# The query multiplication of the first 14 gathered key tiles moved from VectorE to GpSimd

## The reference, cut to what matters

```python
idx = indexer_topk(qi, wi, ki_all, qpos, n_keep)            # n_keep = 256 per sample token
k_sel = jnp.where(is_new, take_rows(k, ni), cache_k[phys, off].astype(k.dtype))
...
logits = jnp.einsum('bqhd,bqkhd->bqhk', q, k_sel).astype(jnp.float32) * ATTN_SCALE + bias
```

## Time and profile before

| | us |
|---|---|
| three runs | 1311.68, 1295.59, 1300.94 (median 1300.94) |
| the profiled execution, its own time | 1294.61 |
| its span | 1292.8 |
| busy: PE / DVE / ACT / POOL | 1150.7 / 779.2 / 309.9 / 188.0 |
| DVE multiplications of key tiles, L1675 | 32, the first starting at 391.5, the last at 659.2 |
| granted TensorE clock, mean | 0.935 of full speed |

### The profile page before, as it was taken

How to read it: one execution, slowest core, us unless ns; L and a number is a source line. 1 busy time by engine, 2 the same in 40 slices (tenths; PEclk the granted TensorE clock), 3 DMA queues, 4 the chain that set the end, 5 groups by cost and what they waited for, 6 DMA issues and landing times.

```text
span 1292.8 us, 16949 instructions
## 1 busy us (share of the span) xinstructions
PE 1150.7 (89%) x6799; PEld 914.6 (71%) x6799; DVE 779.2 (60%) x1561; ACT 309.9 (24%) x638; POOL 188.0 (15%) x202
## 2 busy tenths in 40 slices
PE   6999899998878796776489999999999999989996
PEld 3668787764657642323235468999999999989995
DVE  4399997777879997656432125338667656551220
ACT  2111233122110233211123231423223222241210
POOL 0101100000012223126664400000000000001012
PEclk9999899999899898786578889999999999999998
DMA  9111530105055345135665533112332332223230
GB/s 307 35 57 40 192 117 1 66 1 175 21 170 199 95 164 174 62 100 159 207 178 196 179 76 98 33 34 69 95 99 67 98 98 66 78 74 98 87 106 26
DMA packets 109496, 135.70 MB, mean 105 GB/s; under 512 B 8117, under 2 KB 76109, under 8 KB 108372
## 3 DMA queue, kind: packets, MB, share of 16 engines
q1 hardware_dynamic: 90517, 76.50, 19.5%
q0 software_dynamic: 13824, 46.91, 11.6%
q10 hardware_dynamic: 5077, 11.20, 2.5%
HBM read 129.06 MB, written 5.54 MB: 104 GB/s over the span
## 4 chain that ended last, share of the span: by engine, by line
PE 70%; DVE 20%; issue 4%; ACT 4%; another core or an unknown queue 1%; DMA 0%; POOL 0%; ACTq 0%; DVEq 0%; POOLq 0%
PE G L1199 12%; PE G L1200 11%; PE G L1201 11%; PE G L737 8%; PE G L757 6%; PE G L972 6%; DVE hT L1385 4%; PE G L1055 2%; PE TB L1082 2%; ACT late L2076 2%; DVE ksel L1675 1%; PE UB L1147 1%; DVE late L1513 1%; PE UB L1071 1%; DVE scoreT L1447 1%
## 5 line engine op out<-in xcount | busy, mean ns | idle before, releaser
L1199 PE MATMUL G<-xnH,whi 128*128 128x274 f32 x704 | 205.3, 292 | 1.1 <-DVE aext L1807 0.7
L1200 PE MATMUL G<-xnL,whi 128*128 128x274 f32 x704 | 203.5, 289 | 0.0
L1201 PE MATMUL G<-xnH,wlo 128*128 128x274 f32 x704 | 202.9, 288 | 0.0
L972 PE MATMUL G<-xnT,wring 128*128 128x280 f32 x512 | 137.2, 421 | 9.1 <-ACT nats L2038 4.9
L1199 PEld LDWEIGHTS G<-xnH,whi 128*128 128x128 f32 x704 | 132.4, 188 | 1.6 <-issue 0.9
L1200 PEld LDWEIGHTS G<-xnL,whi 128*128 128x128 f32 x704 | 133.3, 189 | 0.1
L1201 PEld LDWEIGHTS G<-xnH,wlo 128*128 128x128 f32 x704 | 133.1, 189 | 0.0
L1747 DVE TENSOR_TENSOR wlo<-wraw,whi 128x2048 fp32r<-128x2048 f32 (+1 forms) x38 | 76.4, 2011 | 90.5 <-ACT whi L2200 89.6
L972 PEld LDWEIGHTS G<-xnT,wring 128*128 128x128 f32 x512 | 97.7, 197 | 44.6 <-issue 12.6
L2327 POOL DMA_INDIRECT ksel<-in_cache_k_dram,gather_row x64 | 72.5, 1132 | 359.2 <-DVE gather_row L1637 187.1
L1199 PE MATMUL G<-hfH,whi 128*128 128x274 f32 x352 | 102.4, 291 | 0.0
(11 more groups left out here) (388 smaller groups left out, 2067.9 us busy)
## 6 DMA issues: line engine op xcount, KB each, us to landing
wraw<-in_w_up_dram SPq DMA_DIRECT2D x44, 512.0 KB, 5.1
wring<-in_w_in_dram SPq DMA_DIRECT2D x8, 2048.0 KB
wraw<-in_w_down_dram SPq DMA_DIRECT2D x16, 704.0 KB, 4.7
qB<-scr_q SPq DMA_DIRECT2D x32, 256.0 KB
wring<-in_w_in_dram ACTq DMA_DIRECT2D x3, 2048.0 KB
wring<-in_w_o_dram SPq DMA_DIRECT2D x2, 2048.0 KB
toep<-scr_toep SPq DMA_DIRECT2D x1, 2432.0 KB, 15.5
wqi<-in_w_in_dram SPq DMA_DIRECT2D x2, 1024.0 KB, 9.6
```

The lines of the kernel that those rows point to most:

```text
L972: last = pe.matmul(out[:, i, 0:b - a], w[:, j, c:c + P], x[:, j, a:b], start=(j == 0), stop=(j == depth - 1))
L1199: pe.matmul(out, w_hi, x_hi, start=start, stop=False)
L1200: pe.matmul(out, w_hi, x_lo, start=False, stop=False)
L1201: return pe.matmul(out, w_lo, x_hi, start=False, stop=stop)
```

## The change

The multiplication of tiles 0 to 13 goes to POOL: `key_scale(i)` waits for the tile's gathers and its query, multiplies in place and raises the new semaphore `key_scaled`. In DVE's program `key_product(i)` of these tiles waits for `key_scaled` and only sums. In POOL's list `key_scale(i-2)` stands right behind `keys(i)` for i = 2 to 15, ahead of the token list's write for i = 8.

```diff
         def key_product(i):
             g = i // 16
-            dve.wait_ge(s_ksel[i % 3], 32 * (i // 3 + 1))
-            dve.wait_ge(s_qb[i % 3], 16 * (i // 3 + 1))
             x = ksel[i % 3]
-            step(dve.tensor_tensor(x[:, :, :], x[:, :, :], qB[i % 3][:, :].unsqueeze(1).to_broadcast([P, 2, 512]), ALU.mult))
+            if i < FIRST_KEYS:
+                dve.wait_ge(S["key_scaled"], i + 1)
+            else:
+                dve.wait_ge(s_ksel[i % 3], 32 * (i // 3 + 1))
+                dve.wait_ge(s_qb[i % 3], 16 * (i // 3 + 1))
+                step(dve.tensor_tensor(x[:, :, :], x[:, :, :], qB[i % 3][:, :].unsqueeze(1).to_broadcast([P, 2, 512]), ALU.mult))
             col = (i % 16) * 8
...
-        for i in range(9):
+        def key_scale(i):
+
+            pool.wait_ge(s_ksel[i % 3], 32 * (i // 3 + 1))
+            pool.wait_ge(s_qb[i % 3], 16 * (i // 3 + 1))
+            x = ksel[i % 3]
+            pool.tensor_tensor(x[:, :, :], x[:, :, :], qB[i % 3][:, :].unsqueeze(1).to_broadcast([P, 2, 512]), ALU.mult).then_inc(S["key_scaled"], 1)
+
+        for i in range(17):
             keys(i)
-        pool.wait_ge(S["tok_done"], 1)
-        pool.dma_start(scr_tok, tokT[:, :]).then_inc(S["tok_stored"], 16)
-        for i in range(9, 17):
-            keys(i)
+            if 2 <= i < FIRST_KEYS + 2:
+                key_scale(i - 2)
+            if i == 8:
+                pool.wait_ge(S["tok_done"], 1)
+                pool.dma_start(scr_tok, tokT[:, :]).then_inc(S["tok_stored"], 16)
```

More of the change, by code:

```diff
@@ L469, in build_in @@
     names = """cols_ready cols_done toep_ready toep_done toep_scr toep_loaded x_sq x_scaled x_trans xn_done qk_nat
-        qk_sq nat_trans nat_done t1_ready t1_done w_diag q_stored ki_trans ki_done sc_ready sc_done newsc_ready
+        qk_sq nat_trans nat_done t1_ready t1_done w_diag q_stored ki_trans ki_done key_scaled sc_done newsc_ready
         seg_ready seg_done pi_ready pi_relu pi_acc cnt_ready bis_ready pi_tail
```

## The result

The changed kernel takes 1316.5 us in the median of four executions (1307.4 to 1323.8), the kernel before 1303.6, also in the median of four (1295.6 to 1311.7). The ratio is 1.012, with a 95% interval of 1.007 to 1.018: slower by 1.2%, less than the 2% line, but beyond the uncertainty, and above the forecast 1302 and its range (1284 to 1315). The profiled execution, the fastest of the four, took 1307.4 us with a span of 1305.6, which is 12.8 more than the span before. All ratios here are of fast executions; the profiled one of experiment 2 was a slow one (1341.1 us), so that only its loop is read. PE's mean granted clock was 0.926 against 0.935.

A forecast was written before the change was run, and what follows sets the result against it. DVE's loop and the ACT counts it awaits were taken to bound the kernel. 2.7 (tiles 1-3) + 3.2 (5-8) - 0.75 (4, 9-12) - 1.26 (tile 0) = plus 3.9 us, on 1298.3: 1302; range 1284 to 1315.

The forecast's parts named there:

- The exclusion: POOL's multiplication and DVE's L1511, L1504, L1523 and L1524 exclude each other, even at 4 elements; L1513 and PSUM-input L1435 don't.
- the small instructions' rival: Four-element L1504, L1523 and L1524 don't wait for POOL: minus 9.8 us, 1288.5; chance 0.20.
- POOL's length: Each of the 14 POOL multiplications of 1024 elements takes 2.20 us, bounds 2.13 and 2.71.
- Tiles 1 to 3: Turns with counting comparisons: L1504 waits 2.15 us, less 1.26 saved, plus 0.9 us a turn, 2.7 in all.
- Gets in behind L1524: In tiles 1 to 3, POOL's multiplication starts behind L1524 at 396.72 and holds until 398.9, delaying L1504.
- Tiles 5 to 8: Turns with `branch_take`: POOL starts ahead of L1523, 2.05 us lost less 1.26, plus 0.8 a turn, 3.2 in all.
- Tile 0: Multiplied long before the loop, saving 1.26 us; its hold beside the making of the lists costs 0, at most 2.2.
- Tiles 4 and 9 to 12: Multiplication waits for the L1511 pair, then L1523 loses 1.1 us; minus 0.15 a turn, minus 0.75 in all.
- in between the pair: Rival: in tiles 4 and 9 to 12 POOL gets between the two L1511, plus 1.0 a turn; 1308; chance 0.13.
- Passing on: From 496 to the end of attention, a gain or loss of DVE's loop is passed on in full.
- The base: The starting time for the 3.9 us: 1298.3, the middle of four executions of the kernel before.

The follow-up runs named there:

- experiment 2: Kernel before, with 12 same-shape POOL multiplications added behind the gathers of tiles 3 to 14, into an unused buffer nothing in the loop waits for; ratio 1.014.
- experiments 3 and 4: Changed kernel with POOL's multiplication delayed to begin beside L1513 (3: 1304.1 us); 4 starts it beside earlier comparisons and moves DVE's sum ahead of L1523 (1290.1 us).
- experiment 5: Changed kernel, but POOL's multiplication waits for its iteration's L1504, so it becomes ready at the L1511 pair; span 1298.6 us in one execution.
- experiment 6: Changed kernel, but POOL multiplies only one of two rows per partition (512 elements), the other half left out; span 1300.7 us in one execution.
- experiment 1: Changed kernel, but POOL multiplies only four elements per partition, the rest left out, all waits kept; 1290.2 us, ratio 0.988.

## Why the prediction was wrong

- **The exclusion: right.** "I take them as their larger kin": L1504 and L1523, with four elements, are held as long as POOL's multiplication lasts (the maxima above; the small instructions' rival is out). L1513 isn't, nor is the sum: the multiplication beside them keeps its 2.35 us and they theirs (experiments 3 and 4). L1435 never lay beside the multiplication in the changed kernel, so its case stays open.
- **POOL's length: nearly right.** 2.36 measured where 2.20 was estimated from the earlier trace rows. That it was the operands seems likely, as the 1024 elements of experiment 2, with other operands, took 2.13, but this wasn't tried apart.
- **Tiles 1 to 3: right in size, 3.25 against 2.7.** The held instruction was L1523, not L1504. Of the 0.55 too little, 3 x 0.16 is POOL's length. "Gets in behind L1524" was wrong, for the reason of the failed step below: L1523 was caught with the gather still running. Here that changed little in size, so the near hit is in part luck.
- **Tiles 5 to 8: right, 2.95 against 3.2.**
- **Tile 0: gained half.** Instead of 1.26 it is 0.69. The hold met an instruction of the lists, which the prediction had put at 0, with 2.2 as its upper bound: L1624 has 0.79 us beside a multiplication at 370.41.

```profile
370.41 2.35 POOL L2362 TENSOR_TENSOR ksel<-ksel,qB 128x1024 f32<-128x1024 f32 x1 [1.12 <-issue]
...
372.04 0.79 DVE L1624 TENSOR_SCALAR chosen<-iota_f,stat 128x256 f16<-128x256 f16 x1
```

- **Tiles 4 and 9 to 12: the step that failed.** "The multiplication waits for it and holds 496.8 to 499.0. L1523, due at 497.94, loses 1.1: minus 0.15." Measured is plus 1.20 to 1.47 a turn, 6.8 us over the five where -0.75 was forecast. This is 7.5 of the 8.4 us by which the sum (3.9, measured 12.3) was short. The step took the order in which the two engines shut each other out for that of the timeline: first the gather to its end, then the multiplication, which finds the pair running and waits. But where the waits of this multiplication are already met, DVE's instructions are shut out from some 0.3 us after the gather's start. With the gather at 480.85, L1504 at 481.15 is still free and the pair at 481.36 is caught; with the gather at 498.52, L1524 at 498.63 is free and L1504 at 498.83 is caught. So the pair never ran ahead of the multiplication. Experiment 5 makes the forecast's own order come true, with POOL waiting for the pair, and there these turns have 7.39 to 7.41 us, close to the 7.5 of the forecast: the price of the order was right, the order was not. In the earlier trace rows the gather had nothing ready behind it, so that the trace of before couldn't show this.
- **The rival "in between the pair"** had nearly the size (plus 1.0 a turn, 9.6 in all) with another mechanism, and experiment 5 excludes it. A forecast of 1308 from it would have been near for the wrong reason.
- **Passing on: right.** 12.3 at sum 12 and at the projections, 12.8 at the end.
- **The base: too low as well.** The 1316.5 lie 14.3 above the 1302.2 that the forecast rounded to 1302. Of these, 9.0 are the sum (the medians differ by 12.9, the forecast had 3.9). The other 5.3 are the base: the forecast stood on 1298.3, and the median of before became 1303.6. The right sum on the forecast's base would have given 1311, and its own sum on the later median 1307.5; both lie inside the range.

Open stays what exactly shuts DVE out 0.3 us behind a gather's start, and why it lasts through the gather with 512 and 1024 elements but not with four (experiment 6). The rows show when DVE is shut out and on what it depends, not what POOL does meanwhile.

## What to carry to other kernels

Moving an elementwise multiplication from VectorE to GpSimd took nothing off VectorE here, because its neighbours there are TENSOR_SCALAR or two-input instructions in SBUF: they are held for what is left of POOL's longer duration (2.36 us against 1.23), four elements as well as the 528 of the earlier trace rows. Look for the stretch in which VectorE reduces or counts, and let a semaphore start POOL's instruction there; together with the sum in its new place that turned +1.2% into -1.2% here. Don't leave such an instruction behind a gather with its waits already met, since then the hold can begin inside the gather.

## What the runs showed of the hardware that was not expected

- A POOL multiplication that is ready while a gather in front of it runs holds DVE for 3.05 us though it lasts 2.36; at half its length 1.97 for 1.27. With four elements the pair in the gather stays free (0.96 us) and POOL waits (0.66 for 0.21). Readied by a semaphore in mid-gather the full multiplication holds nothing that already runs, and waits itself (2.83 us).
- A one-input TENSOR_SCALAR of 128x1024 in f32 took 2.80 us on POOL, the two-input TENSOR_TENSOR 2.36. It lets DVE through on the way (L1523 with 1.23 us, L1524 free, L1504 with 1.52), which the two-input one did nowhere in the turns read here.
- Two L1511 without a wait between them keep POOL out for both: the multiplication has 2.83 us in experiment 5, and the one of four elements in experiment 1 has 0.66 and ends at 456.65, just behind the pair (456.60). Where DVE had to wait for ACT first (L1523 in the turn to tile 6), POOL's multiplication was already running and DVE was the one held.
